# One projection pass with weights stationary, instead of two with tokens stationary, in a hybrid NSA and Mamba-2 layer

## The reference

```python
def project(x, W):
    p = rmsnorm(x, W['norm_mix']) @ W['w_in']        # 1024 x 2592
    q, kv, gate, z, xbc, dt_raw = jnp.split(p, ...)
    q = rmsnorm(q per head of 64, W['q_norm'])
    kc, vc, ks, vs, kw, vw = split(kv, 6)            # 2 heads of 64 each
    ks, kw = rmsnorm(ks, W['k_norm']), rmsnorm(kw, W['k_norm'])
def causal_conv(xbc, buf, w, b):                     # width 4, 768 channels
    out = b + sum(xp[:, k:k + L] * w[k] for k in range(4))
    return silu(out), xp[:, L:]
```

## Time and profile before

| | |
|---|---|
| median of three runs | 2174.31 us (2172.48 to 2175.98) |
| the profiled execution | 2188.44 us |
| its span, first to last instruction | 2186.7 us |
| TensorE busy, 11632 products | 1904.8 us (87%) |
| VectorE, ScalarE, GpSimd busy | 836.7, 786.8, 311.1 us |
| mean granted clock | 0.925 |

### The profile page before, as it was taken

How to read it: one execution, slowest core, us unless ns; L and a number is a source line. 1 busy time by engine, 2 the same in 40 slices (tenths; PEclk the granted TensorE clock), 3 DMA queues, 4 the chain that set the end, 5 groups by cost and what they waited for, 6 DMA issues and landing times. The chain is left out here.

```text
span 2186.7 us, 31090 instructions
## 1 busy us (share of the span) xinstructions
PE 1904.8 (87%) x11632; PEld 1516.8 (69%) x11632; DVE 836.7 (38%) x1864; ACT 786.8 (36%) x1610; POOL 311.1 (14%) x387
## 2 busy tenths in 40 slices
PE   3986798499998759499898598799999999799899
PEld 2874686366666537365455386799999999778586
DVE  3342331276565476445535334111121111333432
ACT  4464211167665433235533345211111121232432
POOL 1000001044333224432425000000000000000000
PEclk9998899599998669699998799899999999999999
DMA  5311511400000100654748412211111120310410
GB/s 153 58 47 61 177 33 24 95 20 11 11 16 6 22 1 19 254 190 138 252 141 278 170 59 72 78 38 58 38 48 48 38 58 19 102 47 31 131 39 22
DMA packets 117779, 169.73 MB, mean 78 GB/s; under 512 B 26676, under 2 KB 79284, under 8 KB 117474
## 3 DMA queue, kind: packets, MB, share of 16 engines
q1 hardware_dynamic: 96274, 97.03, 15.1%
q0 software_dynamic: 19920, 70.61, 9.7%
q10 hardware_dynamic: 1472, 0.59, 0.2%
HBM read 147.63 MB, written 18.47 MB: 76 GB/s over the span
## 5 line engine op out<-in xcount | busy, mean ns | idle before, releaser
L2414 PE MATMUL banks<-u_parts,w_parts 128*128 128x352 f32 x3168 | 506.7, 322 | 9.4 <-DVE w_parts L2428 9.4
L2414 PEld LDWEIGHTS banks<-u_parts,w_parts 128*128 128x128 f32 x3168 | 506.4, 189 | 9.6 <-issue 9.6
L317 PE MATMUL banks<-w_in_parts,u_parts 128*128 128x512 f32 (+5 forms) x1296 | 275.1, 372 | 28.5 <-DVE w_in_parts L503 24.0
L317 PEld LDWEIGHTS banks<-w_in_parts,u_parts 128*128 128x128 f32 (+1 forms) x1296 | 216.3, 186 | 80.8 <-DVE w_in_parts L503 18.1
L2560 PE MATMUL banks<-w_down_hi,g_parts 128*128 128x512 f32 (+1 forms) x792 | 250.4, 394 | 19.3 <-DVE g_parts L2584 19.2
L2436 DVE TENSOR_TENSOR gT<-silu_gate,banks 128x352 f32 (+1 forms) x66 | 34.4, 521 | 417.9 <-PE banks L2414 417.9
L2560 PEld LDWEIGHTS banks<-w_down_hi,g_parts 128*128 128x128 f32 (+1 forms) x792 | 143.1, 181 | 63.9 <-DVE w_down_lo_b L2581 20.2
L1868 ACT ACTIVATE turned<-banks 128x512 f32<-128x512 f32 (+1 forms) x136 | 79.0, 590 | 184.8 <-PE banks L1733 149.1
L1745 PE MATMUL banks<-turned,cmp_w 128*128 128x512 f32 x256 | 135.1, 610 | 6.2 <-DVE turned L1870 4.3
L2584 DVE TENSOR_TENSOR g_parts<-gT,g_parts 128x256 fp32r<-128x256 f32 (+1 forms) x198 | 78.0, 402 | 156.4 <-ACT g_parts L2543 156.3
L2543 ACT ACTIVATE g_parts<-gT 128x256 fp32r (+2 forms) x198 | 77.0, 398 | 167.9 <-PE banks L2560 167.9
(11 more groups left out here) (380 smaller groups left out, 2496.7 us busy)
## 6 DMA issues: line engine op xcount, KB each, us to landing
w_raw<-in_w_gate SPq DMA_DIRECT2D x22, 512.0 KB, 3.9
w_raw<-in_w_up SPq DMA_DIRECT2D x22, 512.0 KB, 5.0
w_down_raw<-in_w_down SPq DMA_DIRECT2D x44, 256.0 KB, 3.4
x_tile<-in_x_prompt SPq DMA_DIRECT2D x16, 512.0 KB, 4.7
w_in_raw<-in_w_in SPq DMA_DIRECT2D x8, 652.0 KB, 4.0
w_in_raw<-in_w_in SPq DMA_DIRECT2D x8, 644.0 KB, 4.3
x_again<-in_x_prompt SPq DMA_DIRECT2D x8, 512.0 KB, 4.2
w_out_raw<-in_w_out SPq DMA_DIRECT2D x8, 512.0 KB, 7.4
```

Source lines behind the costliest of these rows:

```text
L317: mm = nc.tensor.matmul(m.bank[3 * (j % 2) + i][0:rows[j], 0:hi_col - lo_col], u[:, j % 2, pa, k, 0:rows[j]], wp[:, pb, k, lo_col:hi_col], ...
L2414: mm = nc.tensor.matmul(m.bank[3 * side + q][:, 0:PIECE], wp[:, i, a, k, :], m.u2[:, b, k, q * PIECE:(q + 1) * PIECE], start=(k == 0 and ( ...
```

## The change

The two passes become one, the roles of the operands are swapped, and the convolution stage goes. All 1056 tokens of u stay in SBUF (`u_parts_mix`), in three pieces of 352. The columns of w_in are cut in 21 blocks of 128 channels (the gates and dt together one of 32): six for the convolution, four of plain K and V rows, four of z, the small one, two of normed keys, four of queries. A block's weights are stationary, tokens are the moving operand, channels come out on partitions. An item is a block and a piece; the first three blocks go piece by piece while u is being made, the rest block by block:

```diff
+    blocks = column_blocks()
+    kind = [x[0] for x in blocks]
+    items = [(b, p) for p in range(3) for b in range(W_RING)] + [(b, p) for b in range(W_RING, len(blocks)) for p in range(3)]
...
+    last_item = {b: i for i, (b, p) in enumerate(items)}
...
+    backs = [b for b in range(len(blocks)) if b in slot_of and kind[b] != CONV]
+    back_groups = ((0, 4), (4, 8), (8, 9))
+    back_at = {b: last_item[b] + (2 if kind[b] == NORM else 1) for b in backs}
+    tokens = lambda p: slice(p * PIECE, (p + 1) * PIECE)
+    needs_tile = (2, 5, 8)
```

Three rings of three hold the weights' parts, the evicted columns and the raw halves (512 rows of 128 columns). SyncE's queue has everything now, the parameters, the doubling of keys and the state outputs too:

```diff
+                def load_w(b, half):
+                    q = 2 * b + half
+                    if q >= 2 * RAW_RING:
+                        parted(sp, q - RAW_RING)
+                    at = 0
+                    for col, width in blocks[b][2]:
+                        src = io.w_in[0, 512 * half:512 * (half + 1), col:col + width].rearrange("(k p) c -> p k c", p=P)
+                        sp.dma_start(raw_of(q)[:, :, at:at + width], src).then_inc(landed(q), 16)
...
+                for j in range(4, n):
+                    load_x(j)
+                load_parameters(sp)
+                for b in range(W_RING, len(blocks)):
+                    load_w(b, 0)
+                    load_w(b, 1)
+                    if b == 5:
                         sp.wait_ge(s.bias_row, 1)
                         sp.dma_start(m.bias_dram, m.biasrow[:, :].unsqueeze(1).broadcast_to([NH, P, BIASW])
                                      ).then_inc(s.bias_stored, 16)
-                    if heads and j == n - 2:
+                    if b == 8:
                         sp.wait_ge(s.bias_stored, 16)
-                        sample_bias_tables(sp)
-                    if not heads and j == 1:
-                        window_caches(sp)
...
+                        sample_bias_tables()
+                    if b == 9:
+                        sp.wait_ge(s.tail_taken, 2)
+                        sp.dma_start(io.p_conv[0, 0, :, :], tail_rows[24:27, :]).then_inc(s.tail_stored, 16)
+                        sp.dma_start(io.s_conv.rearrange("o b k c -> (o b k) c"), tail_rows[0:24, :]).then_inc(s.tail_stored, 16)
+                        window_caches()
+                    done = b - 4
+                    if done in slot_of and kind[done] in (ROWS, NORM):
+                        for i in range(3):
+                            store_back(done, i)
+                    if kind[done] == NORM and done in slot_of:
+                        double_keys(blocks[done][1] // 2 - 1, done)
```

TensorE, for each item; four banks turn, so item i waits for the eviction of item i - 4:

```diff
+                def product(i, k):
+                    b, p = items[i]
+                    w = wp[:, b % W_RING, :, k, :]
+                    bank = m.bank[i % 4]
...
                     for pa, pb in TERMS:
...
+                        mm = nc.tensor.matmul(bank[:, 0:PIECE], w[:, pb, :], u[:, pa, k, tokens(p)],
                                               start=(k == 0 and (pa, pb) == TERMS[0]),
                                               stop=(k == KT - 1 and (pa, pb) == TERMS[-1]))
...
+                def head_sums(i):
+                    x_ = norms.index(i)
+                    pe.wait_ge(s.squared, x_ + 1)
+                    if x_ >= 1:
+                        pe.wait_ge(s.rooted, x_)
+                    nc.tensor.matmul(SUMS[:, 0:PIECE], c("head_ones"), sq[:, x_ % 2, :], start=True,
...
+                for i, (b, p) in enumerate(items):
+                    if i >= 4:
+                        taken(pe, i - 4)
+                    for k in range(KT):
+                        if i < 3 * W_RING and k % 4 == 0:
+                            pe.wait_ge(s.u_ready, 2 * needs_tile[p] + k // 4 + 1)
+                        if p == 0 and k % 4 == 0:
+                            parted(pe, 2 * b + k // 4)
+                        mm = product(i, k)
+                        if k == 3 and (i, 0) in turn_at:
+                            turn_x(turn_at[i, 0])
+                    mm.then_inc(s.projected, 1)
+                    if (i, 1) in turn_at:
+                        turn_x(turn_at[i, 1])
...
+                    if i - 1 in norms:
+                        head_sums(i - 1)
+                    for b2 in backs:
+                        if back_at[b2] <= i < back_at[b2] + 3:
+                            turn_back(b2, i - back_at[b2])
+                head_sums(N - 1)
```

ScalarE makes HI of a block's weights behind the last item of the block three before, and in the same list evicts the convolution's items and copies back what TensorE has turned to token rows:

```diff
+                    if b >= W_RING and half == 0:
+                        act.wait_ge(s.projected, last_item[b - W_RING] + 1)
...
+                def take_conv(i):
+                    b, p = items[i]
+                    act.wait_ge(s.projected, i + 1)
+                    if b >= EV_RING and p == 0:
+                        act.wait_ge(s.conv_done, 2 * (b - EV_RING + 1))
+                        act.wait_ge(s.tail_kept, b - EV_RING + 1)
...
+                        act.wait_ge(m.params_in, 16 * N_PARAMS)
+                    nc.scalar.activation(m.xc[:, b, 0:SEQ], ev[:, slot_of[b], 0:SEQ], ACT.Identity,
+                                         bias=m.convb[:, b:b + 1], scale=m.convw[:, 0, b:b + 1])
...
+                for i, (b, p) in enumerate(items):
+                    if kind[b] == CONV:
+                        take_conv(i)
+                    if i < 3:
+                        statistics(6 + i)
+                    if kind[b] == NORM:
+                        square(i)
+                    if i - 1 in norms:
+                        roots(i - 1)
+                    for b2 in range(W_RING, len(blocks)):
+                        if last_item[b2 - W_RING] == i:
+                            w_hi(b2, 0)
+                            w_hi(b2, 1)
+                    if i == back_at[backs[4]]:
+                        act.wait_ge(s.conv_done, 2 * 6)
+                        for b2 in range(6):
+                            y = nc.scalar.activation(m.xc[:, b2, :], m.xc[:, b2, :], ACT.Silu)
+                        y.then_inc(s.silu_done, 1)
+                    for b2 in backs:
+                        if back_at[b2] <= i < back_at[b2] + 3:
+                            copy_back(b2, i - back_at[b2])
+                roots(N - 1)
```

GpSimd makes LO of u and of the weights, VectorE takes the taps of the convolution, evicts the other items and norms the heads with a reciprocal of 352 columns:

```diff
+                def keep_tail(b):
+                    pool.wait_ge(s.tapped, b + 1)
...
+                for j in range(4, n):
+                    u_lo(j)
+                for b in range(W_RING, len(blocks)):
+                    if b - W_RING < 6:
+                        keep_tail(b - W_RING)
+                    w_lo(b)
...
+                    for k in range(1, 4):
+                        y = nc.vector.scalar_tensor_tensor(m.xc[:, b, 0:SEQ], slot[:, k:k + SEQ], m.convw[:, k, b:b + 1],
+                                                           m.xc[:, b, 0:SEQ], ALU.mult, ALU.add)
...
+                    dve.wait_ge(s.rooted, x_ + 1)
+                    chain(nc.vector.reciprocal(r, r))
```

906 lines of the change are left out of this document (471 added, 435 removed).

## The result

| | before | after |
|---|---|---|
| median | 2173.39 us | 2077.54 us |
| all runs | 2166.68 to 2175.98 (4) | 2076.63 to 2082.53 (4) |
| ratio | | 0.9568, 95% interval 0.9541 to 0.9595 |
| profiled execution, span | 2188.44, 2186.7 us | 2076.63, 2074.8 us |

The change makes the kernel 4.3% faster. The forecast was 2093 us with a range of 2058 to 2120; its rival (a) stood at 2066. The profiled execution of before, 2188.44 us, lies 12 us above the slowest of its four runs; that of after is one of its four. On a second chip, where before takes 2190.28 us, the changed kernel took 2108.46, ratio 0.9613 (0.9586 to 0.9640), which is -82 us where the first pair shows -96.

What follows compares the result with a forecast made beforehand. Bound: TensorE inside a projection pass, otherwise start-up, waits and half clock, with stages in series behind barriers. Projection -43, pointwise -6 and convolution -32.5 sum to -81.5 us, from 2174.3 to 2093 us; 2058 to 2120 holds 8 in 10.

Steps and rivals of the forecast that it cites:

- rival (a): Projection: the queue does not hold the weights back, so waits of 15.5 and 11 us fall away; 2066 us, chance 0.22.
- TensorE's sum: Projection: 1488 products at 234.7 us plus transposes, head sums, small pieces and tails; 262.6 us.
- Start: Projection's beginning: first product at 22 us (18 to 27), then 8 us for half clock and two short waits.
- Bias store: Before item 16: weight block 6, queued behind the 1.5 MB store, lands late; 13 us wait plus 2.5 at half clock.
- Cache copies: Near item 25: two 2 MB copies ahead of weight block 10; 8 us wait (0 to 12) plus 3 at half clock.
- Tail: Behind the projection's last product: head sum, root, two reciprocals of 1.9 us and scalings; 6.6 us, lower bound 3.8.
- Sum of the projection: All projection terms, 329.7 us with semaphore waits, plus 3.2 us barrier: next stage at 333 us instead of 375.6, -43 us.
- Pointwise stage: Convolution-state stores and their wait leave, doubled keys no longer load there, compression weights must still land; -6 us (-2 to -12).
- Convolution: The whole 32.8 us stage goes, two VectorE subtractions enter the state-space prologue, its work is covered beside products; -32.5 us.
- (b): Projection items: more starvation from interleaved engine lists, one us more per block, 20 us; 2113 us, chance 0.15 with low clock.
- (c): Projection: weight loads become the bound at 8.9 us per half block; +46 us, 2220 us, chance 0.03.
- (d): Projection: stationary operand is not the saving; a clock kept at 0.93 costs 16 us; counted inside the starvation rival, together 0.15.

Runs made afterwards that it cites:

- one-pass run: Changed kernel with squares and ones matrix as rounded values, so the 18 head sums are one-pass products: 2073.02 us, ratio 0.9577; projection 328.1 us.
- the wide store: Changed kernel with the bias row made on 128 partitions and the 1.5 MB store reading from 128 instead of 8: 2089.61 us, ratio 0.9527.
- 319.5 us projection: Changed kernel with only the bias store reading from 128 partitions instead of 8: 2089.61 us, ratio 0.9527.
- 310.1: Changed kernel with bias store from 128 partitions and cache copies in four: 2073.43 us, ratio 0.9470.
- 304.4: Changed kernel with bias store from 128 partitions, cache copies in four and rounded one-pass head sums: 2047.82 us, ratio 0.9480.
- filler: Changed kernel with thirteen products of constants, result unread, on TensorE in the pointwise stage: 2079.76 us, ratio 0.9612.
- after again: The changed kernel profiled once more on a second chip, no edit: 2108.46 us, ratio 0.9613.
- half of the doubled keys back: Changed kernel with the second partition half of the doubled keys (1 MB) loaded again in the pointwise stage: 2109.31 us, ratio 0.9641.
- the split copies alone: Changed kernel with the two 2 MB cache copies made four of 1 MB, one behind each of weight blocks 9 to 12: 2094.45 us, ratio 0.9542.

## Why the prediction was right, point by point

**TensorE's sum.** 262.6 us was right within 6 us. From the first product to the end of the last item are 300.8 us. TensorE is idle in 25.0 of them and busy 15.2 at half clock, which loses 7.6; that leaves 268.2. Items are 3.84 us instead of 3.79, and the head sums 0.62 us each (4.46 - 3.84), as forecast and as the one-pass run confirms. The waits and the half clock, 32.6 us together, were forecast at 38.5 (8 + 15.5 + 11 + 1 + 3). The two errors nearly cancel, and that part of the hit is luck.

**Start.** First product at 22.68 us (22 forecast). The four waits for the next x tile (1.2, 0.9, 1.7 and 1.4 us) and 5 us at half clock (12 products in 3.89 us, then 2.17) are 7.7 us, so the term of 8 us was right. But item 7 ended at 60.83 + 2 x 3.84 = 68.5 us, not at 63. The forecast's own terms (22 us, eight items, the transposes of x, the 8 us) already give 65 us, so its 63 was worked out too early, and the store's place with it.

**Bias store.** The place and the size of the hole were right, and everything was 5.6 to 7.5 us later: issued at 74.96 instead of 67.5, weights in at 110.1 instead of 104, item 16 at 111.9 instead of 106.3. The choice between a landing of 6.1 us and a long one decided 13 us, and the wide store, worth 16.5 us where the forecast had 15.5, shows that the long one was right. Rival (a) fell. Of the mechanism one step was not right: the forecast has the block wait because it is queued directly behind the store. The landing of 34.3 us agrees with that, and with the sentence "by its rule block 6 lands behind the whole store". But with the store in another queue the hole was 17.35 us, so that order is not what the wait hangs on. The 8 partitions that the store reads are, and the forecast had not looked at them.

**Cache copies.** 11 us forecast (8 and 3 at half clock), 10.6 measured by taking them apart; in after the hole is 6.4 us. The 1 us for the six SiLUs was not measured by itself.

**Tail.** 6.6 us forecast. The last item's products end at 323.5 us, VectorE's last instruction at 330.7: 7.2 us, and the barrier behind it took 4.3 us instead of 3.2. The estimate of 5 ns per column was low, it is (2352 - 179)/348 = 6.2. The reciprocal takes 4.5 times a plain instruction of 352 columns (521 ns), and the run without it shows that VectorE did not bound the last items. The estimate of 4 us from the repeat count in the Trainium skill ("VectorE: DVE Perf Modes", section "Walkthrough: the 8-slice pipeline in each mode") was too high; the measured 2.35 us decides.

**Sum of the projection.** 333 us forecast, 335.0 and 335.9 measured.

**Pointwise stage.** The step that failed in size: -6 us, measured -13.2 and -14.0. I had counted the stores and the wait behind them, which are 3.2 and 5.7 us of it, and said that the compression weights "must land all the same". They do, but before they shared the DMA engines with 2 MB of doubled keys, and without these SyncE was through with its loads 10.0 and 8.3 us earlier. The profile of before had said it: for the second half of the weights SyncE's issues of two 256 KB loads took 7.5 us, and that of a 16 KB load 8.8. My lower bound of -12 was just short.

**Convolution.** -32.5 forecast, -32.8 measured for the stage; the state-space stage did not become longer by the two subtractions (95.5 us instead of 96.0 and 97.1; up to 97.1 in other runs of the changed kernel). Its work beside the products was covered, since TensorE ran ten items of it at 3.84 us without a gap.

**The rest.** "Everything behind is unchanged" is right for the code. The stages give -85 to -87 us and the second chip's medians -82; the first pair's medians say -96, and its profiles -112, of which the sample attention is 26.6 us. By the stages that difference belongs to the executions compared, though its cause is open. The forecast of -81.5 us is 5 us short of the stages' sum, which is the pointwise stage's 7 us less 2 us in the projection; the other 9 us up to the first pair's -96 are not explained by any term of it. That the second chip has -82 is no better proof of the terms.

**Rivals.** (b) and (c) fell: no starvation beyond the start's four waits and the two holes, and a half block of weights lands in 3.3 us in the median of 29, not in 8.9. (d) fell with them: the granted clock of the projection is 0.96 in after, 0.99 without the holes.

## What to carry to other kernels

Before a transfer is put ahead of loads that somebody waits for, read from a trace how long it holds the engines, not only when the first thing behind it lands; and look at the partitions that it reads, since the same bytes from 128 partitions landed in 7.6 us and from 8 in 34. A stage whose issuing engine needs many microseconds for a few loads is worth looking at for its transfers: here 1 MB moved back into it cost 6.9 us. A large copy that nobody waits for cost 10.6 us in one piece ahead of the weights, and nothing that showed once it was cut so that the lead of the loads behind it covered it. And compare unchanged stages first: if they differ between two profiles, that difference is not the change's.

## What was not expected of the hardware

- A store of 1.5 MB from 8 partitions showed a DMA share of 0.51 for 34 us, and of 0.54 when another queue issued it; from 128 partitions it took 7.6 us.
- With a shorter projection the stages behind it did not become faster, and in some runs slower: the prompt attention took 334.1 us behind the 319.5 us projection and 331.9 behind 310.1, but 325.3 behind 304.4, at mean granted clocks of 0.86, 0.87 and 0.89. The granted clock, low from the end of the projection or the pointwise stage on (with one rise in the compression at most, where no filler ran), is at full again 17 to 18 us into the attention in nine profiles, among them before, after and the 304.4 us projection. In after again, behind the 319.5 and 310.1 us projections and with half of the doubled keys back it is so only 34 to 35 us into it, and behind the split copies alone 25. These last five have an attention of 328.4 us and more, the nine others 324.6 to 326.4, except for 328.9 with the filler. What sets the moment stays open; keeping TensorE busy in the pointwise stage did not bring it forward (18 us).
- The sample attention took 335 to 339 us in some groups of runs and 354 to 363 in others, for all kernels of a group alike; the cause was not tried.
